# A kernel of two transformer-like blocks: masked scores kept in PSUM, GpSimd's order in the scan, a twice folded Fourier product and one more ring place

## What is computed

```python
def fourier_mix(u):                      # 256 of the features, in 4 groups of 64
    ug = u.reshape(b, L, N_FGROUPS, FGROUP_DIM)
    yf = jnp.fft.fft2(ug, axes=(1, 3), norm='ortho').real
...
def ssd_scan(xdt, dA, Bm, Cm, h0, with_output):   # chunks of 128 tokens, 12 heads in 4 groups
    st = jnp.einsum('bcsgn,bcsgr,bcsgrp->bcgrpn', Bq, jnp.exp(a_end[:, :, None] - a_cs), xq)
    def step(h, inp):
        s_c, a_c = inp
        return jnp.exp(a_c)[..., None, None] * h + s_c, h
...
    y = y + xs * d_skip                  # then gated, normed, concatenated with fourier_mix, @ w_out
...
def expert_block(args):                  # 64 experts, 2 per token, in two layers
    xb, e = args
    return (jax.nn.silu(xb @ w1[e]) * (xb @ w3[e])) @ w2[e]
```

## Time and profile before

| | us |
|---|---|
| median of the runs (three) | 3248.6 |
| the profiled execution, its own time | 3244.68 |
| its span | 3242.9 |
| TensorE, VectorE, ACT, GpSimd busy | 2760.5, 1510.6, 963.4, 343.3 |
| scan block, about | 394 to 600 |
| mixer output's Fourier product | 604 to 634 |
| expert stages, about | 2015 to 2525 and 2665 to 3180 |

### The profile page before, as it was taken

How to read it: one execution, slowest core, us unless ns; L and a number is a source line. 1 busy time by engine, 2 the same in 40 slices (tenths; PEclk the granted TensorE clock), 3 DMA queues, 4 the chain that set the end, 5 groups by cost and what they waited for, 6 DMA issues and landing times. The chain is left out here.

```text
span 3242.9 us, 42206 instructions
## 1 busy us (share of the span) xinstructions
PE 2760.5 (85%) x16277; PEld 1786.0 (55%) x16277; DVE 1510.6 (47%) x2391; ACT 963.4 (30%) x1713; POOL 343.3 (11%) x388
## 2 busy tenths in 40 slices
PE   5999867797999999999999986798878766988785
PEld 3678767575888878865555575233323552333222
DVE  3148856558777766754555556011111670111114
ACT  6112355235233325445334432011000440111014
POOL 0000057300000000120101000111100001111000
PEclk9999988998999999999999997899989878999998
DMA  7511122322233238540000124999999759999996
GB/s 299 205 52 39 39 111 87 117 65 78 98 105 104 104 127 269 188 167 7 7 7 4 53 96 194 413 400 423 424 425 417 265 201 392 397 424 424 424 420 270
DMA packets 199418, 676.35 MB, mean 209 GB/s; under 512 B 42327, under 2 KB 83742, under 8 KB 145454
## 3 DMA queue, kind: packets, MB, share of 16 engines
q1 hardware_dynamic: 180782, 640.02, 50.5%
q0 software_dynamic: 18432, 33.60, 2.7%
HBM read 626.93 MB, written 80.15 MB: 218 GB/s over the span
## 5 line engine op out<-in xcount | busy, mean ns | idle before, releaser
L3207 PE MATMUL psum<-moe_ring,hreg 128*32 128x512 f32 x2976 | 481.4, 633 | 87.5 <-DMA moe_ring<-in_moe_w 49.3
L3207 PEld LDWEIGHTS psum<-moe_ring,hreg 128*32 128x32 f32 x2976 | 145.8, 116 | 385.2 <-issue 317.6
L3207 PE MATMUL psum<-x,hreg 128*32 128x512 f32 x896 | 319.7, 645 | 12.0 <-DMA moe_ring<-in_moe_w 12.0
L3312 DVE TENSOR_TENSOR ex_hb<-ex_sil,psum 128x256 f32<-128x256 f32 x64 | 27.0, 421 | 571.6 <-ACT ex_sil L3285 571.6
L3259 PE MATMUL psum<-moe_ring,hreg 128*32 128x512 f32 x1344 | 227.2, 612 | 16.6 <-issue 15.2
L1379 PE MATMUL psum<-gu_hi,x1r 128*128 128x512 f32 x712 | 226.5, 394 | 9.3 <-DVE x1r L1506 5.1
L1732 PE MATMUL psum<-dn_op 128*128 128x512 f32 x924 | 210.3, 389 | 4.8 <-DVE dn_op L1827 4.8
L1732 PEld LDWEIGHTS psum<-dn_op 128*128 128x128 f32 x924 | 173.2, 188 | 41.9 <-DVE dn_op L1827 6.0
L3285 ACT ACTIVATE ex_sil<-psum 128x256 f32<-128x256 f32 x64 | 24.5, 383 | 561.7 <-PE psum L3207 561.7
L1379 PE MATMUL psum<-gu_hi,gu_er 128*128 128x512 f32 x504 | 158.5, 389 | 0.0
L1379 PEld LDWEIGHTS psum<-gu_hi,x1r 128*128 128x128 f32 x712 | 135.4, 190 | 39.3 <-DVE gu_lo L1502 7.9
(11 more groups left out here) (613 smaller groups left out, 5817.8 us busy)
## 6 DMA issues: line engine op xcount, KB each, us to landing
moe_ring<-in_moe_w SPq DMA_DIRECT2D x256, 1024.0 KB, 9.3
x<-in_moe_w SPq DMA_DIRECT2D x96, 1024.0 KB
moe_top<-in_moe_w SPq DMA_DIRECT2D x24, 1024.0 KB
x<-in_w_down SPq DMA_DIRECT2D x77, 256.0 KB, 2.9
x<-midrow SPq DMA_DIRECT2D x77, 256.0 KB, 3.4
XF<-in_w_ada SPq DMA_DIRECT2D x16, 1024.0 KB, 5.8
moe_ring<-yrow SPq DMA_DIRECT2D x16, 1024.0 KB, 11.4
xrow<-x SPq DMA_DIRECT2D x24, 512.0 KB, 3.0
```

Of the source, the lines that this page charges most:

```text
L3207: last = pe.matmul(ps[i][r, :], xT[i][:, k, r], place[HOME[n, j]][:, kk * 512:(kk + 1) * 512], start=k == 0, stop=k == KD - 1)
L3312: dve.tensor_tensor(hb[i][:, :], sil[q % 2][:, :], ps[i][:, DE:2 * DE], ALU.mult).then_inc(hbd, 1)
```

## The change

It does five things. (1) Projections: u is folded a second time, so that the positions fall into four classes of 256 columns; V has eight tiles as before, in the order 0, 1, 2, 3, 4, 6, 5, 7, and the two last classes are made by VectorE from an evicted tile and one in PSUM (`V_JOINED`). (2) Mixer output: the table has four tiles of 512 KB, all with places, and the 32 products have 256 columns; ACT writes the first two results out after half of the stage. (3) Scan: the scores are masked in place in PSUM and M reads them there; context tiles have places of their own, so that only three tiles are turned ahead of the cumulative sums and seven between the context's units; the first state of each direction is copied, not decayed and added, and the last one of each is not made; the D-skip product of a chunk is made one unit ahead, in the loop; GpSimd's order in a unit is XW of the next, decay, XDT of the next, sum. (4) Ring: 19 places instead of 18, with another order of seats. (5) The scratch for DMA descriptors is set to 8192 bytes.

```diff
-IN_RING, AT_HOME, AT_TOP = 13, 4, 1
-SEATS = (0, 1, 2, 3, 9, 10, 11, 8, 4, 5, 12, 14, 6, 7, 15, 16, 13, 17)
+IN_RING, AT_HOME, AT_TOP = 13, 4, 2
+DMA_SCRATCH = 8192
+SEATS = (0, 1, 2, 3, 9, 10, 11, 8, 4, 13, 5, 6, 7, 14, 15, 16, 12, 17, 18)
...
@@ projections, TensorE @@
-                for t in range(NT):
-                    if t >= 2:
-                        pe.wait_ge(v_ev, t - 1)
+                for n, t in enumerate(V_TILES):
+                    if n >= 2:
+                        if n - 2 in V_JOINED:
+                            pe.wait_ge(v_join, V_JOINED.index(n - 2) + 1)
+                        else:
+                            pe.wait_ge(v_ev, sum(1 for x in range(n - 1) if x not in V_JOINED))
...
@@ projections, VectorE @@
-                    dve.tensor_tensor(uT[:, m, 0:512], uT[:, m, 0:512], ps[2 * m + 1][:, :], ALU.add).then_inc(u_ev, 1)
+                    dve.tensor_tensor(uT[:, m, 0:512], uT[:, m, 0:512], ps[2 * m + 1][:, :], ALU.add)
+                    dve.drain()
+                    dve.tensor_tensor(quarter[m], uT[:, m, 0:256], uT[:, m, 256:512], ALU.subtract)
+                    dve.drain()
+                    dve.tensor_tensor(uT[:, m, 0:256], uT[:, m, 0:256], uT[:, m, 256:512], ALU.add).then_inc(u_ev, 1)
...
+                for i, n in enumerate(V_JOINED):
...
+                    dve.wait_ge(v_ev, 5 + i)
+                    dve.wait_ge(v_mm, n + 1)
+                    dve.tensor_tensor(three_c, one_c, other_s, ALU.subtract)
+                    dve.tensor_tensor(three_s, one_s, other_c, ALU.add)
+                    dve.drain()
+                    dve.tensor_tensor(one_c, one_c, other_s, ALU.add)
+                    dve.tensor_tensor(one_s, one_s, other_c, ALU.subtract).then_inc(v_join, 1)
...
@@ ssd, TensorE @@
-                for n in range(NT):
+                for n in range(NTC + 1):
                     to_tokens(n)
...
+                pe.wait_ge(ready, 1)
+                pe.wait_ge(cs_ok, 1)
+                n = NTC + 1
                 for u in range(NUC):
+                    for _ in range(2 if u < NUC - 1 else NTT - n):
+                        to_tokens(n)
+                        n += 1
                     stage_b(u)
...
@@ ssd, GpSimd @@
+                weighted(0)
+                weighted(1)
+                for u in range(NUC):
+                    if u >= NDIR:
+                        decay(u)
+                    if u + 2 <= NUC:
+                        weighted(u + 2)
+                stepped(NUC)
+                for u in range(NUC, NU):
+                    t = units[u][1]
+                    if u + 1 < NU - NDIR:
+                        weighted(u + 1)
+                    if u < NU - NDIR:
+                        decay(u)
+                    if u + 1 < NU:
+                        stepped(u + 1)
+                    pool.wait_ge(yo_v, xi(u) + 1)
+                    pool.wait_ge(yd_v, xi(u) + 1)
+                    pool.tensor_tensor(Y[:, t, :], Y[:, t, :], tmp[:, :], ALU.add).then_inc(y2, 1)
...
@@ ssd, VectorE @@
-                    dve.tensor_tensor(SCM[u % 2], ps[n % 2][:, :].rearrange("p (g q) -> p g q", q=P), tri, ALU.mult).then_inc(a_v, 1)
+                    dve.tensor_tensor(scores(n), scores(n), tri, ALU.mult).then_inc(a_v, 1)
...
-                                      SCM[u % 2].unsqueeze(2).to_broadcast([P, NG, HPG, P]), ALU.mult).then_inc(m_ok, 1)
+                                      scores(xi(u)).unsqueeze(2).to_broadcast([P, NG, HPG, P]), ALU.mult).then_inc(m_ok, 1)
...
                     if u > NUC:
                         stage_b(u - 1)
+                        if xi(u) < NT:
+                            first_rows(u)
...
@@ mixer_output @@
-                for n in range(NT):
-                    if n >= NDFT:
-                        sp.wait_ge(four, n - NDFT + 1)
-                    sp.dma_start(dft[:, n % NDFT], dft_dram[n]).then_inc(dft_in[n % NDFT], 16)
+                for n in range(NDFT):
+                    sp.dma_start(dft[:, n], A["dft"][n]).then_inc(dft_in[n], 16)
...
-                            last = pe.matmul(ps[2 * m + odd][:, :], V[:, n, m * 256 + c * P:m * 256 + (c + 1) * P],
-                                             dft[:, n % NDFT, c, :], start=t == 0 and c == 0, stop=t == 3 and c == 1)
+                        for t in range(2):
+                            for c in range(2):
+                                last = pe.matmul(ps[2 * m + odd][:, half * 256:(half + 1) * 256],
+                                                 V[:, 2 * n + t, m * 256 + c * P:m * 256 + (c + 1) * P],
+                                                 dft[:, n, t, c, :], start=t == 0 and c == 0, stop=t == 1 and c == 1)
...
-    nc = bacc.Bacc("TRN2", target_bir_lowering=False, num_devices=1)
+    nc = bacc.Bacc("TRN2", target_bir_lowering=False, num_devices=1, dynamic_dma_scratch_size=DMA_SCRATCH)
```

More of the change, by code:

```diff
@@ L361, in projections @@
         accc = [sb(f"accc{s}", [P, LC]) for s in range(2)]
+        V_TILES, V_JOINED = (0, 1, 2, 3, 4, 6, 5, 7), (5, 7)
+        quarter, v_join = [accc[m][:, :] for m in range(2)], K.sem("pj_vjoin")
         gate = [pad[s][:, :, :].rearrange("p r n -> p (r n)") for s in range(2)]
@@ L722, in ssd @@
     units = [(d, (fwd, bwd)[d][i]) for i in range(NTT) for d in range(2)]
[L723 to L728, removed]
+    NU, NUC, NDIR = len(units), 2 * NTC, 2
+    turns = [NT + c for c in range(NTC)] + list(range(NT))
     with ExitStack() as ctx:
@@ L862, in to_tokens @@
                     for b in range(2):
[L863 removed]
+                        last = act.activation(tokens(turns[n], b * 512, (b + 1) * 512), ps[3 * (n % 2) + b][:, :], ACT.Copy)
                     last.then_inc(ev_a, 1)
[L866 removed]
+                for n in range(NTC + 1):
                     to_tokens(n)
@@ L885, in _ @@
                 pool.memset(ones[:, :], 1.0).then_inc(one, 1)
-                for d in range(2):
-                    last = pool.memset(Hs[d][:, :], 0.0)
-                pool.drain()
                 pool.wait_ge(ready, 3)
@@ L901, in weighted @@
[L901 to L911 removed]
+                    xs, w = scaled(u, W)
@@ L965, in state @@
                     dve.wait_ge(st_mm, u + 1)
-                    dve.wait_ge(dec, u + 1)
+                    if u < NDIR:
+                        for b in range(2):
+                            last = dve.tensor_copy(Hs[d][:, b * 384:(b + 1) * 384], ps[6 + b][:, 0:384])
+                        last.then_inc(st_v, 1)
+                        return
+                    dve.wait_ge(dec, decayed(u))
                     for b in range(2):
@@ L3596, in moe @@
         R.ctx.close()
-        for i in range(AT_TOP):
-            with nc.sbuf_tensor(f"moe{layer}_top{i}", [P, PIECE], F32, side="right") as under:
-                K.place.append(under[:, :])
+        with ExitStack() as under:
+            for i in range(AT_TOP):
+                K.place.append(under.enter_context(nc.sbuf_tensor(f"moe{layer}_top{i}", [P, PIECE], F32, side="right"))[:, :])
         E = Memory()
```

154 lines of the change are left out of this document (84 added, 70 removed).

## The result

| | before | after |
|---|---|---|
| median of the runs, us | 3247.93 (4 runs, 3245.12 to 3250.39) | 3168.03 (4 runs, 3167.18 to 3170.74) |
| ratio | | 0.9758, 95% interval 0.9745 to 0.9771 |
| the profiled execution, own time / span | 3244.68 / 3242.9 | 3168.71 / 3166.8 |
| TensorE, VectorE, ACT, GpSimd busy | 2760.5, 1510.6, 963.4, 343.3 | 2729.9, 1494.3, 964.1, 315.9 |

The account below looks back on a forecast made before the run. Bounds differ by stage: a cycle of waits in the scan, TensorE in the Fourier product, weights' DMA in the expert stages. -40 - 18 - 14.6 + 2.2 - 9 = -79.4 takes the 3248.6 median to 3169 us, range 3154 to 3199.

Parts of the forecast that it names:

- Steady part: Scan units: GpSimd's cycle falls from 9.84 to 6.86 us, the 15 gaps from 147.6 to 108; -40 us.
- the term of 0.9 us: First seven scan units: a D-skip product makes GpSimd's sum wait some 0.9 us, giving 7.75 us per unit.
- TensorE as the next bound: Scan units: TensorE needs 6.55 us per unit at full clock, closely behind GpSimd's cycle of 6.86.
- Prologue: Scan start: fewer token tiles and D-skip products ahead bring the first Y add earlier; -18 us, bounds -14 and -21.
- Fourier: Fourier product: 32 products of 256 columns instead of 512, -14.2 us; with evictions inside the stage, -14.6.
- projections: Projections: the second fold's VectorE operations and joined V tiles cost +2.2 us, bounds +1.2 and +3.5.
- Ring: Expert stages: one more 1 MB place for weights shortens the dips in their DMA stream; -9 us, bounds 0 and -9.5.
- what the first dip gives back moves the second's end forward too: Expert weights' DMA: savings in a layer's two dips add, 1.7 + 2.47 in layer 0, 2.47 + 2.47 in layer 1.
- Scratch: Indirect DMAs: halving the descriptor scratch to 8192 bytes costs nothing.
- Rival 4: Indirect DMAs on GpSimd's queue wait for descriptor space, costing 147 us at 1.15 us each: 3316; chance 0.02.
- Rival 1: Scan: TensorE leads at half clock, 4 of 15 units slow at 12.4 us, +20, prologue -14: 3193; chance 0.13.
- the bound for a blocked XW: Scan units: if M's time and XW's blocking stay, 1.55 x 15 comes back, leaving -16 us.

Follow-up runs that it names:

- experiment 1: The changed kernel with the masked scores put in SBUF again and read there by product M; 3192.65 us, ratio 0.9838.
- experiment 4: The changed kernel with GpSimd's order decay, XW, XDT, sum, and the second decay ahead of the first unit's XW; 3161.93 us, ratio 0.9739.
- ring18: The changed kernel with 18 places for the experts' weights and the old order of seats, scratch still 8192 bytes; 3173.24 us, ratio 0.9771.
- stream_longer: The changed kernel with nine small memsets more on GpSimd at the scan's start; 3167.34 us, ratio 0.9754.
- scratch_only: The kernel before with only the DMA descriptor scratch set to 8192 bytes; 3246.83 us, ratio 1.0006.

## Why the prediction was right, point by point

**Steady part, -40 against -41.1.** The mechanism was right. The decomposition of GpSimd's cycle held to 0.02 us: 6.86 forecast, 6.88 measured, 8.31 with the old order (6.88 + 1.43). M at 1.74 and XW at 1.47 are the values taken, and experiment 1 shows what makes them so. The Trainium skill's rule (SBUF — State Buffer, on who interferes with whom) agrees with the trace in kind: by it the early units would be 7.75 and without it 7.3, and they are 7.46, nearer to the second, but the blocking is there in every one of the seven sums (2.40 against 1.82). Mis-sized was the term of 0.9 us, which measured 0.6, as the sum starts 0.2 us late anyway: 7 x 0.3 = 2 us. The last three gaps are 6.27, 6.44 and 5.73, against 6.86, 6.3 and 6.3; the kernel before's own last gap was 8.36, where the forecast had 9.84. So both sums were too long, by 2.9 us after and 1.4 before.

**TensorE as the next bound** was mis-sized: 6.55 us per unit, from distances of starts, is more than it needs, as 6.28 without a wait in experiment 4 shows. Nothing hung on it, because GpSimd led.

**Prologue, -18 against -19.7** (-21.6 in the second trace). The tiles gave 6 to 8 us (6.2 forecast). Eight D-skip products ahead take 8.05 us in the old kernel and 11.11 in the new one, where GpSimd is at work beside them; the changed kernel has one of 1.20 there, 6.9 less than the old. No run gives the rest of this term, the context's copies and decays, by itself.

**Fourier, -14.6 against -14.1, projections +2.2 against +2.8.** Over ten traces with the fold the stretch from the first subtraction to the scan is 212.6 us on average, over three without 209.9: +2.7. So the projections' term was 0.5 us too small, inside its bound of +3.5; the second fold itself takes 2.0 of it (1.8 forecast). What the forecast did not see is that this part comes to 8.2 us in the new scan and to 2 and 5 in the old one by the medians, with the start of the old scan 6 to 8 us longer in both of its traces: the parts of this change do not seem to add simply.

**Ring, -9 against -9.1: right in total by two errors.** The step that failed is "what the first dip gives back moves the second's end forward too", which made it 2.47 us in three dips and 1.7 in one. `ring18` shows about 5 us for the place: 1.5 to 2.8 in layer 0, 2.7 in layer 1, which is about once 2.47 per layer, in the second dip. The rest of layer 1's 6.5 us, 3.8, came with the new scan: GpSimd's stall stood ahead of layer 1's first gather, and the shorter scan moved it behind that gather, so that the first product began earlier and the first dip nearly went. Of these 3.8 us `stream_longer` gives back 2.5 in the trace; the other 1.3 are open. That the total is 9.1 is luck.

**Scratch, 0 against 0**, shown by `scratch_only` within 0.2%. Rival 4 is out.

**Rival 1** (half clock) appeared in single units and in the first products of the scan, some 2 us each, and not as a mode. The start of the program, 2.2 us later in the first trace, is the same code, and the first subtraction lies between 180.8 and 188.7 us in fourteen traces: no part of the change.

Two figures on record are off by a microsecond: the bound for a blocked XW is -40 + 15 x 1.55 = -17, not -16, and the forecast's own bounds give 3161 to 3174, not 3162 to 3176. Nothing hangs on either.

## What to carry to other kernels

Where two engines share a path to SBUF, look at which operand of the longest instruction can stay in PSUM: here keeping one 128x512 operand in PSUM was worth 25 us, more than the reordering of the whole unit (16 us), each measured with the other in place. Write the cycle of a loop as a sum of distances from one unit's rows, engine by engine, and ask of each piece whether it must stand ahead of the next hand-over; the same sum pointed to the decay first, which shortened the later units from 6.88 to 6.28 us. And test a forecast's terms even when its total is right: one of these was right only because an unrelated stall had moved.

## What the runs showed that I had not expected

- A GpSimd stall of several microseconds moves with the instructions ahead of it in its program: nine memsets 2200 us earlier move it ahead of a gather (7.1 us late, as the 6.9 to 7.3 with the old scan), and without them it is behind it (1.8, then 3.6 to 4.4 us idle before the second).
- The same 14 us saved on TensorE late in the block came to 8.2 us in one kernel and 2 and 5 us in another, where a stretch 200 us earlier ran longer at half clock (1.2 GHz). Why it did is open.
- VectorE's D-skip product lengthens a GpSimd sum that starts 0.2 us after it by 0.6 us, and eight of them in a row grow from 8.05 to 11.11 us when GpSimd works beside them.
- The spread of one kernel's executions is itself not steady: the kernel before lay within 20.4 us in one set of 23 runs (3237.37 to 3257.75), and within 5.3 to 8.0 us in the four other sets, of 4 to 15 runs.
